# The triangular inverse of a chunked RWKV-7 scan: sixty-four-wide products replaced by 128x128 transposes, and a new order of the scan's stages

## The reference, cut to what matters

```python
def step(state, inp):
    r_t, w_t, k_t, v_t, kk_t, a_t = inp
    sa = jnp.einsum('bhvk,bhk->bhv', state, -kk_t)
    state = (state * w_t[:, :, None, :] + sa[..., None] * (kk_t * a_t)[:, :, None, :]
             + v_t[..., None] * k_t[:, :, None, :])
    return state, jnp.einsum('bhvk,bhk->bhv', state, r_t)
```

## Time and profile before

| what | value |
|---|---|
| median of 3 runs | 2973.12 us |
| the profiled execution, its own time | 2974.16 us |
| its span in the profile | 2972.4 us |
| matmul engine (PE) busy | 2735.3 us, 92% |
| VectorE (DVE) busy | 1471.6 us, 50% |
| ScalarE (ACT) busy | 1214.0 us, 41% |
| GpSimd (POOL) busy | 409.9 us, 14% |
| the scan's iterations | from about 2065 to 2550 us |

### The profile page before, as it was taken

One profiled execution on the slowest core, in us unless ns is written; L12 is line 12 of the kernel. 1 busy time (PEld: TensorE's weight loads), 2 busy tenths in 40 slices (PEclk: granted clock), 3 DMA queues, 4 the chain that ended last, 5 costly groups with the idle time before them and its releaser, 6 DMA issues. The chain is left out here.

```text
span 2972.4 us, 56808 instructions
## 1 busy us (share of the span) xinstructions
PE 2735.3 (92%) x24888; PEld 2159.4 (73%) x24888; DVE 1471.6 (50%) x2295; ACT 1214.0 (41%) x2071; POOL 409.9 (14%) x332
## 2 busy tenths in 40 slices
PE   6999999999999999898889999799778876899999
PEld 5877557688878888785578888676666655678887
DVE  2532774744443333526554243886566764453343
ACT  3332564632242222325543232665446644442232
POOL 1001451000000000103100000001435443100000
PEclk9998999999999999999999999899999999899999
DMA  4222002133222222232222222230000001222221
GB/s 160 94 82 85 1 1 92 71 128 113 100 85 99 92 99 99 81 123 66 68 94 99 91 100 99 78 118 24 7 7 8 8 7 34 114 93 99 85 99 71
DMA packets 38821, 228.84 MB, mean 77 GB/s; under 512 B 4352, under 2 KB 8448, under 8 KB 15024
## 3 DMA queue, kind: packets, MB, share of 16 engines
q1 hardware_dynamic: 32576, 201.34, 18.9%
q0 software_dynamic: 6000, 23.87, 2.4%
HBM read 220.93 MB, written 4.26 MB: 76 GB/s over the span
## 5 line engine op out<-in xcount | busy, mean ns | idle before, releaser
L447 DVE TENSOR_TENSOR weights_lo<-ring,weights_hi 128x1024 fp32r<-128x1024 f32 x353 | 435.5, 1236 | 700.2 <-ACT weights_hi L440 700.1
L440 ACT ACTIVATE weights_hi<-ring 128x1024 fp32r<-128x1024 f32 x364 | 382.2, 1053 | 577.5 <-PE bank L577 335.3
L2519 PE MATMUL bank<-scan_low,scan_low 64*64 64x64 f32 x4608 | 106.0, 233 | 55.4 <-DVE scan_low L2934 33.4
L496 PE MATMUL bank<-mlp_h_hi,weights_hi 128*128 128x512 f32 x384 | 151.3, 394 | 2.0 <-DVE mlp_h_lo L792 2.0
L497 PE MATMUL bank<-mlp_h_lo,weights_hi 128*128 128x512 f32 x384 | 151.0, 393 | 0.0
L498 PE MATMUL bank<-mlp_h_hi,weights_lo 128*128 128x512 f32 x384 | 150.7, 393 | 0.0
L496 PE MATMUL bank<-h_hi,weights_hi 128*128 128x512 f32 x384 | 150.0, 391 | 0.0
L575 PE MATMUL bank<-weights_hi,mlp_p_hi 128*128 128x512 f32 x384 | 149.6, 390 | 0.0
L497 PE MATMUL bank<-h_lo,weights_hi 128*128 128x512 f32 x384 | 149.4, 389 | 0.0
L577 PE MATMUL bank<-weights_hi,mlp_p_lo 128*128 128x512 f32 x384 | 149.4, 389 | 0.0
L576 PE MATMUL bank<-weights_lo,mlp_p_hi 128*128 128x512 f32 x384 | 149.4, 389 | 0.0
(11 more groups left out here) (666 smaller groups left out, 6774.8 us busy)
## 6 DMA issues: line engine op xcount, KB each, us to landing
ring<-in_w_m SPq DMA_DIRECT2D x64, 1024.0 KB, 4.6
ring<-in_w_mb SPq DMA_DIRECT2D x24, 1024.0 KB, 4.5
ring<-in_w_fi SPq DMA_DIRECT2D x22, 1024.0 KB, 4.6
ring<-in_w_fo SPq DMA_DIRECT2D x10, 1024.0 KB, 4.8
ring<-in_w_a SPq DMA_DIRECT2D x7, 1024.0 KB, 4.8
attn_bias<-scratch POOLq DMA_DIRECT2D x16, 448.0 KB, 4.5
ring<-in_w_rg SPq DMA_DIRECT2D x5, 1024.0 KB, 5.0
ring<-in_w_v SPq DMA_DIRECT2D x4, 1024.0 KB, 15.3
```

Of the source, the lines that this page charges most:

```text
L440: act.e.activation(halves(g, s)[0], raw, ACT.Copy).then_inc(*act.up("act_unit_high", ("high", s)))
L447: lane.e.tensor_tensor(lo, raw, hi.bitcast(F32), ALU.subtract).then_inc(*lane.up(f"{lane.name}_unit_low", ("low", s)))
L496: pe.e.matmul(ps[:, :], hi, xh, start=k == 0, stop=False, skip_group_check=True)
L2519: m = pe.e.matmul(out[to], left[rows], right[rows], start=start, stop=stop, skip_group_check=True)
```

## The change

**In the scan's inverse.** The transposed running inverse of levels 1 to 4 is no longer a product. After X of a level has been copied to SBUF, `pe_turned_pairs` transposes it with 8 transposes of 128x128 (two units of two heads in each). For this X and Y are laid out so that a pair of units is a 128x128 block: `pe_to_pairs` writes y, `pe_to_heads` writes x, each by 32 single 64x64 matmuls whose quadrants follow one another in another sequence than before. The last level's xt stays a product. LM x X of the next level is issued ahead of the transposes.

**Stages and table.** The operand rows become a fifth stage (`r`), padding yields are gone, and `ORDER` is written anew for all four engines. The counts of how much of the first head is issued early (`EARLY`) are given for each engine.

**Gate weights** are split before the blocks of w_kv instead of after them. **w_va** joins w_a2's group, so that its first units are split in the run of w_a2, and all low parts by VectorE.

```diff
-GROUPS = (... ("w_fi0", "w_fo0", "w_fi1", "w_fo1"), ("w_a2",), ("w_va",), ("w_ao",), ...
+GROUPS = (... ("w_fi0", "w_fo0", "w_fi1", "w_fo1"), ("w_a2", "w_va"), ("w_ao",), ...
...
+    for dst, src in ((L.maskb, g.tri), (L.identb, g.ident)):
+        act.e.activation(dst, src, ACT.Copy).then_inc(*act.up("act_masks", ("nsa_masks",)))
+    act.wait_ge(g.at("gate_w_loaded"))
+    high_part(g, act, "gate_w", L.gw, L.gws)
     for what, i in gemm_steps("w_kv", NB, range(8)):
...
+def pe_quarter(pe, ps, n, left, right, start, to):
+    rows, into = slice(64 * start, 64 * start + 64), slice(64 * to, 64 * to + 64)
+    return pe.e.matmul(ps[into, n * CH:(n + 1) * CH], left[rows], right[rows], start=True, stop=True, skip_group_check=True)
+def pe_to_pairs(g, pe, key, left, right):
+    banks = [bank(g, pe, key + (a,)) for a in range(2)]
+    for u in range(2 * NCH):
+        for a in range(2):
+            m = pe_quarter(pe, banks[a], u // 2, left[:, u, :], right[:, u, :], a, u % 2)
+def pe_to_heads(g, pe, key, left, right, cross):
+    banks = [bank(g, pe, key + (j,)) for j in range(2)]
+    for u in range(2 * NCH):
+        for a in range(2):
+            n = u // 2 * 2 + a
+            m = pe_quarter(pe, banks[u % 2], u // 2, left[:, n, :], right[:, n, :], u % 2, a ^ cross(u % NCH))
+def pe_turned_pairs(g, pe, key, src):
+    banks = [bank(g, pe, key + (j,)) for j in range(2)]
+    for n in range(NCH):
+        m = pe.e.transpose(banks[n // 4][:, n % 4 * P:(n % 4 + 1) * P], src[:, 2 * n:2 * n + 2, :].rearrange("p a t -> p (a t)"), g.ident)
...
-ORDER = {"pe": "mmmhthathahhmmttamammamahthamattmammamamamamtamamhhamatmtamhtatmhhhtahmamamamththhama",
+ORDER = {"pe": "mmaarmmartamhamammarmmatmarmahamahamrmhaamaammattamaammaammmaa",
...
-    for level in range(1, 6):
-        LM = R.LM[level % 2]
...
-        pe_pass(g, pe, ("xt", b, level), xt_sides(level), R.Y, lambda u: XT[:, u, :])
+    for level in range(2, 6):
+        for j in range(2):
+            pe.wait_ge(g.at("masked", b, level, j))
+            pe.wait_ge(g.at("x", b, level - 1, j))
+        pe_to_pairs(g, pe, ("y", b, level), R.LM[level % 2], R.X)
+        yield
+        pe_turned_pairs(g, pe, ("xt", b, level - 1), R.X)
+        yield
+        for j in range(2):
+            pe.wait_ge(g.at("y", b, level, j))
+            pe.wait_ge(g.at("xt", b, level - 1, j))
+        if level < 5:
+            pe_to_heads(g, pe, ("x", b, level), XT, R.Y, lambda c: 0)
+        else:
+            pe_to_heads(g, pe, ("xt", b, level), R.Y, XT, upper)
         yield
```

More of the change, by code:

```diff
@@ L1853, in act_attn_in @@
                 drain_copy(g, act, ("w_a2", i), A.kT[:, i - 8, :] if i < 12 else A.vbT, ps[:, :])
-    for s in first_units("w_va"):
-        act_unit(g, act, s)
     for i in range(QT):
@@ L1926, in pool_attn_in @@
         pool_attn_bias(g, pool, n)
-    for s in first_units("w_va"):
-        low_unit(g, pool, s)
     end(g, pool, "attn_in")
@@ L2274, with early @@
 BESIDE = {0: (1, 2), 2: (4, 3), 3: (5, None)}
-EARLY = 11
-def early(first, nb):
-    for _ in range((nb + 1) * EARLY // NB - nb * EARLY // NB):
+EARLY = {"pe": (0, 1, 1, 1, 2, 3, 3, 3), "act": (1, 1, 2, 3, 5, 8, 8, 12), "dve": (0, 1, 1, 1, 2, 3, 5, 7)}
+def early(lane, first, nb):
+    done = EARLY[lane.name]
+    for _ in range(done[nb] - (done[nb - 1] if nb else 0)):
         next(first, None)
@@ L2470, in dve_rwkv_in @@
                 low_unit(g, dve, i)
-    for _ in range(3):
+    for _ in range(4):
         next(first)
@@ L2491, in pool_rwkv_in @@
     pool.wait_ge(g.at("head_consts"))
-    for _ in range(13):
+    for _ in range(2):
         next(first)
@@ L2553, in side_bank, with by_two, side_of @@
-def side_bank(kind, ps):
-    if kind == "half":
-        return ps.rearrange("p (d c t) -> p d c t", d=2, c=4)
-    if kind == "pair":
-        return ps.rearrange("p (e b t) -> p e b t", e=4, b=2)
-    return ps.rearrange("p (d g x) -> p d g x", d=2, g=2)
-def pe_pass(g, pe, key, kind, left, right, flip=0):
-    sides = [[8 * d + c for d in range(2) for c in range(NCH) if SIDES[kind](c) == j] for j in range(2)]
+def by_two(ap, j):
+    return ap.rearrange("p (n j) t -> p j n t", j=2)[:, j]
+def side_of(j, ap):
+    return ap.rearrange("p (d j c) t -> p j d c t", d=2, j=2)[:, j]
@@ L2565, in pe_pass @@
+def pe_pass(g, pe, key, left, right, flip=0):
+    sides = [[8 * d + c for d in range(2) for c in range(NCH) if upper(c) == j] for j in range(2)]
     banks = [bank(g, pe, key + (j,)) for j in range(2)]
@@ L2591, in stages @@
                 pass
-def quanta(n):
-    for _ in range(n):
-        yield
 def pe_head(g, pe, b):
@@ L2744, in pool_head @@
     R = g.R
-    yield from quanta(11)
     if b >= 3:
@@ L2775, in pe_middle, with act_rows, dve_rows, pool_rows @@
         yield
+    banks = [bank(g, pe, ("tv", b, j)) for j in range(2)]
+    for i in range(4):
+        for j in range(2):
+            c = 4 * j + i
+            m = pe_heads(pe, banks[j][:, i * CH:(i + 1) * CH], R.vT[:, b, c * CH:(c + 1) * CH], R.centre, cross=j)
+    m.then_inc(*pe.up("pe_tokens", ("filled", ("tv", b, 0)), ("filled", ("tv", b, 1))))
+    yield
+    for e in range(2):
+        ps = bank(g, pe, ("bonus", b, e))
+        pe.wait_ge(g.at("bonus_in", b))
+        pe.e.matmul(ps[:, :], g.bd, R.kd[:, e, :], start=True, stop=True, skip_group_check=True).then_inc(
+            *pe.up("pe_head", ("filled", ("bonus", b, e))))
+    yield
+def act_rows(g, act, b):
+    R, o = g.R, b % 2
+    if b >= 2:
+        act.wait_ge(g.at("advanced", b - 2))
+    fours = R.TBK[o].rearrange("p (q x) t -> p q (x t)", x=4)
+    for d in range(2):
+        for j in range(2):
+            key = ("tbk", b, d, j)
+            dst = fours[:, 2 * d:2 * d + 6:5] if j else fours[:, 2 * d + 1:2 * d + 5:3]
+            drain_copy(g, act, key, dst, filled(g, act, key)[:, :].rearrange("p (a x) -> p a x", a=2), key)
+            yield
+    for j in range(2):
+        key = ("tv", b, j)
+        drain_copy(g, act, key, R.TV[o][:, 4 * j:4 * j + 4, :], packed(filled(g, act, key)[:, 0:256]), key)
+    yield
+def dve_rows(g, dve, b):
+    R = g.R
+    for e in range(2):
+        ps = filled(g, dve, ("bonus", b, e))
+        dst = (R.kT, R.vT)[e][:, b, :]
+        if e:
+            dve.wait_ge(g.at("filled", ("tv", b, 1)))
+            dve.wait_ge(dve.newest)
+        dve.e.tensor_tensor(dst, R.vT[:, b, :], ps[:, :], ALU.mult).then_inc(
+            *dve.up("dve_middle", ("bonus", b), ("drained", ("bonus", b, e))))
+        yield
+def pool_rows(g, pool, b):
+    pool_scaled_eye(g, pool, b, 1)
+    yield
+def pe_middle(g, pe, b):
+    R, o = g.R, b % 2
+    AR, XT = R.AR[b % 3], R.XT[o]
+    for d in range(2):
+        pe.wait_ge(g.at("bb", b))
+        pe.wait_ge(g.at("kb", b))
         pe.wait_ge(g.at("minus_kk", b))
@@ L2966, in pool_middle @@
             *pool.up("pool_middle", ("xt", b, 0, d)))
-        masked(1, d)
-    yield from quanta(2)
-    for d in range(2):
-        masked(2, d)
         yield
-    yield from quanta(2)
-    for d in range(2):
-        masked(3, d)
-        yield
-    yield
-    for level in range(2, 6):
-        yield
-        for d in range(2) if level < 4 else ():
-            masked(level + 2, d)
-        yield from quanta(2 if level < 5 else 1)
-    yield
+    for level in range(1, 6):
+        for d in range(2):
+            masked(level, d)
+            yield
 def pe_advance(g, pe, b):
@@ L3086, in pe_tail @@
     pe.mark("wg_read", b)
-    yield from quanta(4)
+    yield
 def y_part(g, b):
```

216 lines of the change are left out of this document (69 added, 147 removed).

## The result

The changed kernel takes 2916.95 us (median of 4 runs, 2916.45 to 2921.04), the kernel before 2972.22 us beside it. The ratio is 0.9817, 95% interval 0.9802 to 0.9833: 55 us faster. Forecast were 2930 us, 2918 to 2946 for the likeliest case, 2906 to 2964 in all.

A forecast was written before the change was run, and what follows sets the result against it. The prediction took the supply of TensorE's instructions, in pieces of 256, as the scan's nearest bound. Terms of 33.6 + 3.5 + 6.0 + 1.0 = 44 us took 2974.16 to 2930 us; likeliest case 2918 to 2946, range 2906 to 2964.

The forecast's parts named there:

- The supply of instructions is the nearest bound of the scan: Scan: TensorE's instructions come in pieces of 256, 3.7 us apart; 14.1 pieces make 52 of an iteration's 56.2 us.
- sum -4.8 per iteration: Scan: three legs of one walked iteration, -4.9, +0.6 and -0.5 us; over seven iterations -33.6 us.
- The first leg: Products to Y of level 2: 5.5 pieces at 3.7 us make 20.4 us instead of 25.3, gain 4.9.
- The transposes in TensorE's own time: Inverse: almost no change, 8 transposes about 0.85 us against 0.95 for a pass of 32 products; 0.4 us deducted per block.
- lower bound of a block's gain: Scan, per block: 1.75 borders between pieces at the mean pause of 0.85 us, less 0.4, so at least 1.1 us.
- The gate weights: Gate weights' matmuls: the 4.16 us wait and 2.3 us of lowered clock go; -6.0 us, between -4.2 and -6.5.
- w_va: First w_va matmul, a 4.32 us wait for VectorE's bias sums: -1 us, with ends of -4.3 and +1.3.
- Pieces are cheap: Scan: pauses only replace other waits, each block gains 1.1 us, 9 in all plus 7 for small edits; 2958 us, chance 0.16.
- The supply is the whole bound: Scan: each block gains the full 7.0 us, 62 us with the other terms; 2912 us, chance 0.14.
- Single quadrants one after another: Inverse: neighbouring 64x64 matmuls exclude one another, 8 passes per block take 1.9 instead of 0.95 us; 2991 us, chance 0.06.
- a pass of over 1.2 us: Sign at L2548's passes that would show single 64x64 quadrants running one after another; about 0.95 us was expected.
- A worse queue: Scan: the new table idles TensorE in leg 2 as much as leg 1 gains, 2967 us, or 2983; chance 0.08.

The follow-up runs named there:

- e9: Kernel before plus both small edits (gate weights, w_va), the transposed product of levels 1 to 4 replaced by 2 matmuls on 256 columns (wrong inverse); 2916.95 us.
- e5: Changed kernel with the 8 transposes of a level turned back into 32 products of 64x64 with an identity, at the same place; 2937.1 us.
- e11: Kernel before with 64 more TensorE instructions, once, ahead of the scan; 2969.0 us, ratio 0.9999.
- e12: Kernel before with 128 more TensorE instructions, once, ahead of the scan; 2970.0 us, ratio 0.9997.
- e8: Changed kernel with six groups of level 0 and 1 products each replaced by one 128x128 matmul on 512 columns (wrong inverse); 2905.7 us.
- e6: Kernel before with the two small edits alone: gate weights split before the w_kv blocks, w_va in w_a2's group; 2964.6 us.
- e7: Changed kernel with the bonus sums moved from behind y of level 2 to ahead of it, by the table alone; 2928.0 us.
- e2: Changed kernel with 2 matmuls of 128x128 on 512 columns added ahead of the transposes of each level; 2955.7 us.
- e1: Changed kernel with 14 units of 64x64 products (112 instructions) added ahead of the transposes of each level; 2960.6 us.

## Why the prediction was right, and where it was off

**The bound.** "The supply of instructions is the nearest bound of the scan": shown for the scan before the change. Taking instructions out at nearly the same array time gave 48 us (e9), putting them back cost 20 (e5), moving the count moved the long iterations (e11, e12), and the pauses stand 256 instructions apart or a multiple of it. Iterations with all their instructions took 51.6 to 54.8 us in the new order, next to the 52 that 14.1 pieces at 3.7 us make; one of 51.6 and one of 52.0 say that 3.7 is a little too long for the distance, and on queue 8 the shortest distances in the scan are 3.3 to 3.5 us.

**The legs.** Means over six iterations, with the forecast worked for one iteration (from the earlier trace rows):

| leg | before, walked | before, mean | forecast after | after, mean |
|---|---|---|---|---|
| products to Y of level 2 | 25.3 | 25.0 | 20.4 | 20.2 |
| Y of level 2 to Y of level 5 | 23.0 | 23.3 | 23.6 | 24.1 |
| Y of level 5 to products | 7.8 | 9.3 | 7.3 | 6.6 |

Each leg of the changed kernel was forecast within 0.7 us, their sum within 0.4. The term of the sum that was mis-sized is "sum -4.8 per iteration": it measured -6.7, and 6 x 1.9 = 11 us is most of the miss of the total. By legs it is -4.8, +0.8 and -2.7 against -4.9, +0.6 and -0.5, so the miss lies in the third. It came from the choice of the iteration that was walked: "56.2 us" stood for all, and the mean was 57.6, with 9.3 us in the third leg instead of 7.8. The other terms held: the stretch before the scan gave 8.4 us (forecast 7), the first iteration 4.2 (3.5), and what follows the last mark 4.7 (4.8). e11 and e12 say why the walk misled: in the old order an iteration's length, 54.8 to 63.7 us for the same code (the first of the six, which has no tail, left out), hangs on where the borders fall, and the walked one was a mild case. The list of all marks stood in the trace of before.

**The first leg came out right for a wrong reason.** Its 4.9 us rest on "5.5 pieces, x 3.7 = 20.4 us", that is, on the supply as the bound of this leg. Here are the first two legs of the iteration that was walked, with the columns of the earlier trace rows, before

```profile
2231.80:2257.20 25.40, 24.08 (x754) 17.90 (x754) 15.68 (x39) 20.41 (x31) 14.19 (x11) 1.00 0.02 4
2257.20:2280.20 23.00, 15.44 (x759) 12.99 (x750) 19.97 (x28) 8.82 (x17) 12.41 (x8) 1.00 0.06 16
```

and after:

```profile
2205.50:2227.20 21.70, 18.71 (x664) 15.25 (x656) 10.74 (x29) 13.22 (x22) 15.01 (x12) 1.00 0.02 4
2227.20:2251.40 24.20, 21.33 (x668) 15.72 (x658) 20.80 (x38) 15.71 (x27) 11.05 (x8) 1.00 0.05 15
```

The same over the six iterations, means in us:

| leg | TensorE busy, before | after | pauses for issue, before | after |
|---|---|---|---|---|
| products to Y of level 2 | 23.3 | 18.1 | 1.2 | 1.1 |
| Y of level 2 to Y of level 5 | 15.7 | 21.1 | 4.3 | 0.2 |
| Y of level 5 to products | 5.5 | 4.9 | 2.4 | 0.7 |

The first leg was full of TensorE's own work before and after, and its pauses stayed. It got shorter because the new table moved 5 us of that work into the second leg. e8 agrees: 349 recorded instructions fewer in this leg, 1.4 pieces or 5 us at 3.7, took off 0.3 us. The second leg took the work and grew by only 0.8 us, because its pauses and some of its waits went. So the supply did pay for the gain, in the second and third leg; the forecast had the amount nearly right and the place wrong, and 20.4 against 20.2 is luck.

**The transposes in TensorE's own time.** Forecast 0.4 us more per block. The page says 0.3 us *less* for the whole kernel with transposes than with products (e5), so the cost does not show in the sum. What e5's text calls the change of mode does show between single instructions of the changed kernel (medians over the six iterations): the first transpose starts 0.15 us after the last 64x64 matmul of the y pass, and the next 64x64 matmul 0.20 us after the last transpose, where one 64x64 group starts 0.04 us after another. Both steps are small against the pauses. The 0.4 us stand in the lower bound of a block's gain and in the first rival's 8 x 1.1; no run shows this term, and what the runs showed in its place are the 0.3 us less and the two steps.

**The share of the order.** The prediction gave the table of stages no share and only a rival for harm. That was right for what the change yields as a whole (e9 reaches the same time without it), and incomplete: had the transposes been left out, the table with its single quadrants would have given 27 us (e6 to e5).

**The gate weights.** Forecast -6.0, and the earlier trace rows has its answer: no wait, 0.23 us steps. **w_va.** Forecast -1, measured -2.2 by the wait. The low part in front of the sums did come, but the sums themselves went faster. VectorE's timeline of before and of after, the small operation between two sums:

```profile
1342.66 1.10 DVE L2099 TENSOR_SCALAR attn_heads<-attn_heads 128x2 f32<-128x2 f32 x1
...
1345.00 1.08 DVE L2099 TENSOR_SCALAR attn_heads<-attn_heads 128x2 f32<-128x2 f32 x1
```

```profile
1336.35 0.17 DVE L2095 TENSOR_SCALAR attn_heads<-attn_heads 128x2 f32<-128x2 f32 x1
...
1337.76 0.17 DVE L2095 TENSOR_SCALAR attn_heads<-attn_heads 128x2 f32<-128x2 f32 x1
```

Both edits together were forecast at 7 us; alone they gave 6.2 (e6).

**The rivals.** *Pieces are cheap* is out: 55 us, not 15. *The supply is the whole bound* came near in the old order, where 1.9 pieces gave 6.2 us of at most 7.5 (e6 to e9). In the new order it did not hold: 1.75 pieces gave 2.2 us of at most 7.0 (e5 to the changed kernel), and 1.4 more gave 1.3 (e8). That the changed kernel's total lies nearly as close to its 2912 as to the forecast's 2930 does not decide between them. *Single quadrants one after another* is out: by it a pass would take 1.9 us (its 0.43 us for 512 columns is also in the trace of before, where the last rows of L2800 start 0.43 us apart), and the 48 passes of L2548 in the six iterations have a median of 0.94 us from first to last start, as passes had before. The sign on record for it, a pass of over 1.2 us, did appear, in 11 of the 48 (1.28 and 1.56 us in the iteration shown; the second has a border in it, with 0.36 us between two starts). It was set too close to the 1.16 us of before. Nor are the x passes, whose neighbours share their rows, slower than the y passes (the fastest take 1.11 us in both, and the median of 0.94 us is the same). *A worse queue* is out, and e7 shows how such a queue looks.

**What stays open.** Why the new order loses only 29 us to pauses with the same number of instructions that cost 43 in the old one. That a level of the old order has nearly two pieces, so that a bad place repeats, fits the long iterations; no run changed only that. And why TensorE's busy time fell by 9 us in e9.

## What to carry to other kernels

Where an engine pauses for "issue" and nothing else, count its instructions between two pauses, and count those that an edit removes: here 448 to 480 instructions per block (matmuls and their weight loads) were worth 20 to 48 us with nearly the same work in the array. Before you put a gain into a leg, look at the busy time of that leg alone: where the engine is full, fewer instructions shorten next to nothing (e8: 360 fewer in a leg of 19.9 us with 18.6 busy took off 0.3 us). Measure a periodic stage over all its periods before walking through one, since its length can hang on a phase (54.8 to 63.7 us here for the same code). And before adding two gains, ask whether they are ways out of the same loss; a square of four kernels answers it.

## What the runs showed of the hardware

- Matmuls of 64x64 in float32 started every 15 ns where neighbours go over all four quadrants (64 in about 0.95 us), and every 28 ns where they use one diagonal pair (62 in 1.76 us, level 1 of this scan, e2). Nothing in the prediction used this, and it spoiled e1.
- In the changed kernel, from the last 64x64 matmul to the first 128x128 transpose TensorE took 0.15 us, and 0.20 us back, where one 64x64 group follows another after 0.04 us.
- TensorE's pauses for issue fell at one place in each 256 of its instructions: all 41 of over 0.5 us in the scan of before stand at 193 or 194 in this count. Each ended 2.2 to 2.9 us after a transfer of 16 KB on queue 8 had begun, and 3584 matmuls and weight loads fewer took 14 of these transfers away.
- Three of the four long iterations also had a lower granted clock: 0.91 in the one of 59.9 us, 0.92 in those of 63.4 and 63.7, against 0.94 to 1.00 in the other middle ones of the same three kernels. TensorE had paused in them for up to 2.3 us at a time. Part of the length of the last two is this: their busy time was 47.7 and 47.1 us, where an iteration at full clock had 44.5. The clock alone does not make an iteration long: the sixth takes 61.2 us at 0.97 before and 61.4 us at 0.92 in e6.
- A VectorE operation on 128x2 elements (L2099) took 0.78 to 1.10 us in its three executions while GpSimd was making low parts (1339.0 to 1346.1 us), and 0.17 us in the fourth, behind them, and in all four after the change.
